# A two-layer hybrid diffusion trunk on one core: the first norm's last token tile is taken by halves, and the other two are modulated, turned and given to the router ahead of it

## The reference

```python
def layer_norm(x, g, b):
    mu = jnp.mean(xf, -1, keepdims=True)
    var = jnp.mean(jnp.square(xf - mu), -1, keepdims=True)
    return ((xf - mu) * lax.rsqrt(var + LN_EPS) * g + b).astype(x.dtype)

# per layer l, for the context tokens and alike for the latent tokens
y = mixer(x * (1.0 + sc1) + sh1, ...)
x = layer_norm(ALPHA * x + g1 * y, ln1_g[l], ln1_b[l])          # the first norm
f = moe_ffn(x * (1.0 + sc2) + sh2, w_router[l], b_router[l], ...)
x = layer_norm(ALPHA * x + g2 * f, ln2_g[l], ln2_b[l])

# moe_ffn, its head
scores = jax.nn.sigmoid((x @ w_router).astype(jnp.float32))
sel = scores + b_router.astype(jnp.float32)
...                                                              # best 4 of 8 groups, best 6 experts
wsel = wsel / jnp.sum(wsel, -1, keepdims=True) * ROUTE_SCALE
...                                                              # each token through its 6 experts, and a shared one
```

## Time and profile before

| | |
|---|---|
| median of 3 runs | 1921.86 us (1921.61 to 1923.24) |
| the profiled execution | 1911.23 us, its span 1909.5 us |
| PE busy | 1694.6 us, 89% of the span |
| DVE, ACT, POOL busy | 854.7, 389.9, 158.5 us |
| mean granted TensorE clock | 0.935 of full speed |
| chain that ended last | PE 34%, DMA 6%, DVE 5%, ACT 1%, issue 1% |
| projection ends / first block's product begins, layer 0 | 324.0 us / 372.9 us |
| the same, layer 1 | 1254.8 us / 1306.1 us |

### The profile page before, as it was taken

The page is one execution under the profiler, slowest core; times in us unless marked ns, Lnnn a source line. Parts: engine busy times, 40 slices in busy tenths (PEclk is TensorE's granted clock), DMA queues, the critical chain, the costliest instruction groups (busy, mean ns, idle before and its releaser), DMA issues. The chain is left out here.

```text
span 1909.5 us, 22774 instructions
## 1 busy us (share of the span) xinstructions
PE 1694.6 (89%) x8463; PEld 917.5 (48%) x8463; DVE 854.7 (45%) x1696; ACT 389.9 (20%) x754; POOL 158.5 (8%) x148
## 2 busy tenths in 40 slices
PE   4999989997999799979779999899979979999783
PEld 1885644643444343434348756455434434444341
DVE  2435425654344343433863444356433434444266
ACT  1323531211111111111122334211111111111111
POOL 0000000230000000000020000015100000000002
PEclk7999989799999899999889999988989999999896
DMA  9534527469989999999234452544798999999950
GB/s 350 170 137 159 198 94 296 183 252 398 397 354 397 411 400 412 397 425 409 84 117 126 143 212 74 226 165 150 296 424 344 394 409 396 420 408 399 423 209 34
DMA packets 103471, 538.98 MB, mean 282 GB/s; under 512 B 36830, under 2 KB 39662, under 8 KB 64060
## 3 DMA queue, kind: packets, MB, share of 16 engines
q1 hardware_dynamic: 91996, 515.24, 68.1%
q0 software_dynamic: 11296, 22.14, 3.1%
q10 hardware_dynamic: 64, 0.07, 0.0%
HBM read 545.95 MB, written 6.59 MB: 289 GB/s over the span
## 5 line engine op out<-in xcount | busy, mean ns | idle before, releaser
L1106 PE MATMUL bank<-ring,arena_a 128*32 128x512 f32 (+2 forms) x2432 | 474.0, 627 | 80.8 <-DMA ring<-in_w_expert_gu 79.9
L1106 PEld LDWEIGHTS bank<-ring,arena_a 128*32 128x32 f32 (+2 forms) x2432 | 164.8, 134 | 357.4 <-issue 356.6
L1682 DVE TENSOR_TENSOR arena_a<-arena_a,bank 128x512 f32<-128x512 f32 x336 | 230.4, 686 | 9.7
L1133 PE MATMUL bank<-arena_b,arena_a 128*32 128x512 f32 (+2 forms) x800 | 212.9, 615 | 18.2 <-DVE arena_a L1671 12.2
L1700 DVE SCALAR_TENSOR_TENSOR arena_a<-arena_a,slot_w,bank 128x256 f32<-128x256 f32 x64 | 30.8, 481 | 442.7 <-ACT arena_a L1968 339.5
L1156 PE MATMUL bank<-ys_hi,to_token 128*128 128x512 f32 x384 | 171.4, 446 | 15.4 <-issue 7.8
L1157 PE MATMUL bank<-ys_lo,to_token 128*128 128x512 f32 x384 | 153.3, 399 | 0.0
L1716 DVE TENSOR_TENSOR ys_lo<-bank,ys_hi 128x512 fp32r<-128x512 f32 x128 | 82.5, 686 | 156.6 <-ACT ys_hi L1976 156.6
L2043 POOL DMA_INDIRECT arena_a<-scratch_x,slot_idx x60 | 61.2, 1019 | 915.9 <-PE bank L1093 859.6
L1968 ACT ACTIVATE arena_a<-bank 128x256 f32<-128x256 f32 x64 | 24.7, 386 | 525.0 <-PE bank L1106 525.0
L1976 ACT ACTIVATE ys_hi<-bank 128x512 fp32r<-128x512 f32 x128 | 69.5, 594 | 273.7 <-PE bank L1133 273.7
(11 more groups left out here) (291 smaller groups left out, 2003.2 us busy)
## 6 DMA issues: line engine op xcount, KB each, us to landing
ring<-in_w_expert_gu SPq DMA_DIRECT2D x128, 2048.0 KB, 13.2
arena_b<-in_w_expert_down SPq DMA_DIRECT2D x88, 1024.0 KB, 17.4
ring<-in_w_mod SPq DMA_DIRECT2D x24, 2048.0 KB, 7.8
arena_a<-in_w_expert_down SPq DMA_DIRECT2D x40, 1024.0 KB, 18.1
ring<-in_w_in SPq DMA_DIRECT2D x10, 2048.0 KB, 12.8
ring<-in_w_out SPq DMA_DIRECT2D x4, 2048.0 KB, 7.8
arena_b<-mods SPq DMA_DIRECT2D x8, 512.0 KB, 9.8
arena_a<-mods SPq DMA_DIRECT2D x8, 512.0 KB, 10.0
```

Of the source, the lines that this page charges most:

```text
L1106: ins = pe.matmul(psum[0][r:r + w, :], xT[:, k, r:r + w], ring_view(gu_slot(n))[:, k, :], start=(k == 0), stop=(k == KD - 1))
L1133: ins = pe.matmul(psum[5 + f][r:r + w, :], hT[b % 2][:, k, r:r + w], down[n % ND][:, k, CH * f:CH * f + CH], start=(k == 0), stop=(k == 1))
L1682: ins = dve.tensor_tensor(z, z, bank[:, :], ALU.add)
```

## The change

The norm's last tile is split off, on four engines.

- DVE: the loop of modulations and the call `norm(0, ...)` go. In their place: statistics of tiles 0 and 1, modulation of tile 0, `scale_shift` of tile 1, the first half of tile 2's sum (`last_half`: gate, ALPHA, `bn_stats`, all over 512 columns), modulation of tile 1, the second half, then mean, variance, `scale_shift` and modulation of tile 2. The modulation's add is two instructions of half the columns each, with a semaphore step for each.
- ACT: norms tiles 0 and 1, copies their turned banks, then norms tile 2 and copies its banks.
- PE: the eight matmuls of `keep_busy` go; two stand ahead of the turning of tile 2. The logits of tile 1 come ahead of that turning. A transpose group waits for its half of `xm2`.
- POOL: waits for the second step of a tile's two.

```diff
@@ turn_x
+                        if which:
+                            pe.wait_ge(xm_ready, 2 * t + g + 1)
                         for k in range(4):
                             ins = pe.transpose(...)
@@ PE, behind the projection
-                keep_busy(("xT", 1, 0, 0), 8)
                 for t in range(2):
-                    pe.wait_ge(xm_ready, t + 1)
                     turn_x(1, t, xm2)
                 pe.wait_ge(wr_loaded, 16)
                 bank = begin(("logit",))
                 logits(bank, 0)
-                pe.wait_ge(xm_ready, TILES)
+                logits(bank, 1)
+                keep_busy(("xT", 1, 2, 0), 2)
                 turn_x(1, 2, xm2)
-                logits(bank, 1)
                 end(logits(bank, 2), ("logit",))
@@ DVE
-                norm(0, from_psum)
-                for t in range(TILES):
+                def modulate(t):
                     c_ = 0 if t == 0 else 1
                     dve.wait_ge(normal_ready, t + 1)
                     link(dve.tensor_tensor(scaled, xm[:, t, :], gain2[:, c_, :], ALU.mult))
-                    dve.tensor_tensor(xm2[:, t, :].rearrange("q (k p) -> q p k", k=KD), scaled.rearrange("q (p k) -> q p k", k=KD),
-                                      add2[:, c_, :].rearrange("q (p k) -> q p k", k=KD), ALU.add).then_inc(xm_ready, 1)
-                    dve.wait_ge(xm_ready, t + 1)
+                    for f in range(2):
+                        ks = slice(4 * f, 4 * f + 4)
+                        dve.tensor_tensor(xm2[:, t, :].rearrange("q (k p) -> q p k", k=KD)[:, :, ks], scaled.rearrange("q (p k) -> q p k", k=KD)[:, :, ks],
+                                          add2[:, c_, :].rearrange("q (p k) -> q p k", k=KD)[:, :, ks], ALU.add).then_inc(xm_ready, 1)
+                    dve.wait_ge(xm_ready, 2 * t + 2)
+                def last_half(n):
+                    bank = done(dve, ("y", 2, n))
+                    cols = slice(CH * n, CH * n + CH)
+                    z = xm[:, 2, cols]
+                    link(dve.tensor_tensor(z, bank[:, :], gateb[:, 1, cols], ALU.mult))
+                    dve.sem_inc(free[groups[("y", 2, n)][0]], 1)
+                    link(dve.scalar_tensor_tensor(out=z, in0=x[:, 2, cols], scalar=ALPHA, in1=z, op0=ALU.mult, op1=ALU.add))
+                    link(dve.bn_stats(bn[:, 6 * n:6 * n + 6], z))
+                statistics(0, 0, from_psum)
+                statistics(0, 1, from_psum)
+                modulate(0)
+                scale_shift(0, 1)
+                last_half(0)
+                modulate(1)
+                last_half(1)
+                link(dve.bn_aggr(bnag[:, 4:6], bn))
+                dve.tensor_scalar(rstd[:, 2:3], bnag[:, 5:6], EPS, None, ALU.add).then_inc(lvar_ready, 1)
+                scale_shift(0, 2)
+                modulate(2)
@@ ACT
-                norm(0)
-                turned()
+                norm(0, 0, 1)
+                turned(0, 1)
+                norm(0, 2)
+                turned(2)
@@ POOL
-                    pool.wait_ge(xm_ready, t + 1)
+                    pool.wait_ge(xm_ready, 2 * t + 2)
```

More of the change, by code:

```diff
@@ L1814, in late_rows, with turned @@
                     act.dma_start(mods[:, n // 2, CH * (n % 2):CH * (n % 2) + CH], stage[n % 2]).then_inc(stage_sent[n % 2], 16)
-                def turned():
-                    for t in range(TILES):
+                def turned(*tiles):
+                    for t in tiles:
                         for g in range(2):
@@ L1930, in _, with norm @@
                     act.sem_inc(yT_ready, 1)
-                def norm(which):
-                    for t in range(TILES):
+                def norm(which, *tiles):
+                    for t in tiles:
                         act.wait_ge(lvar_ready, TILES * which + t + 1)
@@ L2015, in _ @@
                 rows_high(NB - 1)
-                norm(1)
+                norm(1, *range(TILES))
             @blk.gpsimd
```

## The result

The changed kernel takes 1888.59 us (median of 4 runs, 1888.09 to 1889.68), the kernel before on the same chip 1921.73 (4 runs, 1918.31 to 1923.24): a ratio of 0.9831, 95% interval [0.9814, 0.9848]. The sign, the mechanism and its size behind the projection were right; 12 us came on top.

What follows compares the result with a forecast made beforehand. A serial chain from output projection to experts was taken as the bound; sigmoids earlier by 9.4 us (layer 0) and 11.4 (layer 1), together 20.8, gave 1921.86 - 20.8 = 1901.1 us, range 1897.5 to 1912.0.

Steps and rivals of the forecast that it cites:

- Before T: DVE ahead of the output projection's end: early modulations and half of tile 2 done 0.9 us before that end.
- The rival of the dear half: DVE's halved modulation add costs as much as a whole: 11.2 us gained, 1910.7 us; chance 0.05.
- Behind T: From the output projection's end to the sigmoid: 12.0 us, gaining 9.4 us in layer 0 and 11.4 in layer 1.
- the rows from 258 us: PE's transposes and 64-column products, 258 to 266 us: clock held at 1.00, so it should hold in the changed stretch.
- the rule that the prediction set against the change: PE losing six of eight idle matmuls: short idles lose the full clock; gain then 10.2 us, rival's chance 0.19.
- Does it last to the end: From sigmoid through the experts: stages start earlier but keep their lengths, so the gain lasts; 1.4 us allowed for drift.
- The experts again 567 to 569: Experts' stretch, up to the last down product's start, stays 567 to 569 us in the changed profile.
- the sum: Whole kernel: sigmoid gains of 9.4 and 11.4 us, together 20.8, taken off the profiled 1911.23 us to 1890.4.
- I have no row for that difference and carry it over: Whole kernel: timed runs lie 10.6 us above the profiled execution, kept unchanged, so 1921.86 - 20.8 = 1901.1 us.
- the two items that it names for its lower end: Range's lower end, 1897.5 us: the cheaper half of DVE's add, 0.35 us twice a layer, and the drift.
- bound by their weights: Experts wait for weight transfers and take the gain back: time stays 1921.9 us; chance 0.06.
- fall out of step: Experts' weight stream shifts against PE, eighteen more blocks run 1.44 us slower: 1927 us; chance 0.03.

Runs made afterwards that it cites:

- the ten passes: Kernel before with ten unread DVE passes between its last modulation and the wait for the sigmoid: 1932.08 us (one run).
- one layer at a time: The change made in one layer only, against the kernel before: layer 0 alone 1904.58 us, ratio 0.9927; layer 1 alone 1904.62 us, ratio 0.9935.
- the delay that took it away: Changed kernel with 14 (layer 0) and 16 (layer 1) idle matmuls in place of 2 ahead of tile 2's turning: 1916.04 us, ratio 0.9984.
- the passes that made the start later: Changed kernel with seven or eleven unread DVE passes ahead of the choice of experts: 1901.72 and 1915.14 us, one run each.
- the kernel before with less code: Kernel before without the six idle matmuls ahead of the attention of layer 0: 1916.40 us (10 runs), ratio 0.9979.
- the changed kernel with the added code: Changed kernel with twelve small unread matmuls, some 48 PE instructions, at the start of layer 0: 1894.18 us (4 runs), ratio 0.9872.

## Why the prediction was wrong in size and right in kind

**Before T.** As predicted: the halved adds cost 0.98 us each (0.97 taken), the second modulation ends 0.9 us ahead of T in both layers. The rival of the dear half falls.

**Behind T.** As predicted: root at T + 3.3 (T + 3.15), sigmoid at T + 12.1 and T + 12.0 (T + 12.0). The two gains are 9.3 and 11.4 us, 20.7 together (20.8). The clock stayed at 1.00, as the rows from 258 us had it; the rule that the prediction set against the change did not decide here, but the run without the two idle matmuls shows its case, 1.7 and 1.8 us a layer. The 2 us by which layer 1 gains more are the clock's and not the order's. In a layer laid out the old way the sigmoid stood at T + 21.4 or, with the last logits at half clock, at T + 23.2 to T + 23.7. All four traces of the kernel before had the latter in layer 1, but one variant (the ten passes) had it in layer 0 as well, and two that were edited in layer 0 alone had it in neither. The prediction carried it over from one profile without asking what sets it; that it held was luck in part.

**Does it last to the end.** The gain did: one layer at a time, by the delay that took it away, and by the passes that made the start later. "The experts again 567 to 569" did not hold. From first product to last down product's start it was 565.5 and 566.6 us. The greater part is PE's code, which the prediction did not think of: with the idle matmuls some of PE's instructions went, and all later ones moved. Against the first trace the experts became 3.3 us shorter in layer 0, of which 1.1 went back before layer 1, and 1.1 in layer 1. Behind the fourth sum, where the code acts, it was 2.2 and 2.4 us; the rest, 1.1 us less in layer 0 and 1.2 us more in layer 1, lies ahead of that sum and stays open.

**The step that failed** is in the sum: "I have no row for that difference and carry it over", the 10.6 us between the profiled execution and the timed runs. It was treated as a constant around the span. But each run's time, in every kernel here, lies only 1.7 to 3.0 us above its own span. The 10.6 us are the scatter of the kernel before, whose profiled execution was a quick one; the changed kernel's runs begin at their profile and end 8.5 us above it. From profile to profile the gain is 23.0 us (1911.23 to 1888.22): 20.7 from the sigmoids and 2.3 from all the rest, the experts' 3.3 (3.3 and 1.1, less 1.1) less what other stages gave back. From median to median it is 33.1, and about 10 of that is the carried difference: the changed kernel's median lies 0.4 us above its profile and not 10.6. On two other chips, with more runs of the kernel before, the medians are 27.8 us apart (1920.61 and 1892.77) and 25.9 (1917.85 and 1891.91). That is still more than 20.8, so a second term was too small: the sum put the experts' change at nothing, where the code alone gave 2.0 us in layer 0 and 2.5 in layer 1 (the means behind the fourth sum over the four and the three traces). With these, 20.7 comes to about 25. The range was too narrow below for both reasons; besides, the two items that it names for its lower end, 1.4 us of halves and 1.4 of drift, make 2.8 us, and it took 3.6.

**The rivals.** The experts were not bound by their weights, since all of the gain arrived; PE's waits for weights in layer 1 stayed (39.4 us, nine, against the earlier trace rows):

```profile
PE bank L1106 <- DMA ring<-in_w_expert_gu: 39.4, 9, 10.0
```

So the stream did not fall out of step either. One reading of the prediction was wrong there: not each of the nine waits let the clock fall. The three of 0.9 to 1.6 us, at 1487.63, 1540.30 and 1733.24 us, stand in stretches of 10 us with a granted clock of 1.00.

Open: whether the changed kernel scatters less than the kernel before, and why it would. The delayed kernel and the kernel before with less code, both with late sigmoids, scattered by 12.6 us in ten runs each, the kernels with one layer by 10.5 in eight and 6.6 in four, the changed kernel with the added code by 7.4 in four. The numbers of runs differ too much for these spans to be compared, and no run shows a cause.

## What to carry to other kernels

Where a chain of norm, modulation and routing stands between two dense stages, do all tiles but the last ahead of the stage's last product, and let PE have their small work while the last tile is finished: here that also kept its clock, and two idle matmuls in the one gap left brought the sigmoid 1.7 us a layer forward. Don't carry the difference between one profile and the timed runs into a prediction as a constant; look at several executions before taking it for overhead. When a stage with unchanged instructions changes its length, look for loads of code ahead of the first late instruction: adding or removing instructions far ahead on that engine moved them here.

## What was not expected of the hardware

- A wait of PE that the profile puts down to DVE lasted 1.2 to 1.8 us longer where loads of code stood beside it, worth some 2.3 us a layer with the clock that fell in it; it came and went with 24 to 48 PE instructions more or less, hundreds of microseconds ahead.
- An idle PE of 5.17 us was followed by 15 us at half clock, in which PE was busy for 13.6 us; one of 2.01 us between small products was followed by 0.51 in the 4.8 us behind it, and with two idle matmuls in that gap the clock stayed at 1.00.
- The same program ran from 1911 to 1933 us, with mean granted clocks from 0.937 to 0.921.
